# Two fused blocks on one core: rotary halves exchanged by DMA, q's root moved into the softmax's scale, low parts in four instructions

## What is computed

```python
def first_block(...):                 # 512 latent and 256 context tokens
    x, xc = rwkv7 layer               # scans in both directions, 16 heads of 64
    x = differential attention layer  # 8 heads, 2 x 64 wide, keys: 256 context + 512 latent
def second_block(...):                # two layers of hybrid_layer
    qa = rope(rms_norm_2(to_heads(a_q, 6), qk_g[0])) ...   # 6 window heads
    qb = rope(rms_norm_2(to_heads(b_q, 6), qk_g[2])) ...   # 6 dilated heads
    qm = rms_norm_2(to_heads(m_q, 4), qk_g[4])             # 4 memory heads, no rope, 256 keys
```

```python
def rope(x):                          # apply_axial_rope: the same in two groups of 2 x 16 channels
    x1, x2 = x[..., :half], x[..., half:]
    return concatenate([x1 * cos - x2 * sin, x2 * cos + x1 * sin])
```

## Time and profile before

| | |
|---|---|
| median of 3 runs | 2569.64 us (2568.6 to 2583.72) |
| profiled execution | 2575.68 us, span 2573.9 us |
| busy in the span | TensorE matmuls 2209.8, weight loads 1631.9, VectorE 1367.8, ScalarE 1156.6, GpSimd 679.5 us |
| mean granted TensorE clock | 0.936 of full |
| chain that ended last, by engine | PE 62%, DVE 15%, ACT 11%, issue 7%, POOL 3%, DMA 2% |
| a high part on ScalarE (line 238) | 128 times, mean 1052 ns |
| stages, about | `Mix` and `Scan` to 1200 us, `Mid` to 1344, `Diff` to 1775, first out-projection to 1857, pages to 2134, out-projection to 2230, pages to 2507, out-projection to 2573.9 |

### The profile page before, as it was taken

The page is one execution under the profiler, slowest core; times in us unless marked ns, Lnnn a source line. Parts: engine busy times, 40 slices in busy tenths (PEclk is TensorE's granted clock), DMA queues, the critical chain, the costliest instruction groups (busy, mean ns, idle before and its releaser), DMA issues.

```text
span 2573.9 us, 59035 instructions
## 1 busy us (share of the span) xinstructions
PE 2209.8 (86%) x25736; PEld 1631.9 (63%) x25736; DVE 1367.8 (53%) x2342; ACT 1156.6 (45%) x1933; POOL 679.5 (26%) x410
## 2 busy tenths in 40 slices
PE   8799999288888878876879999996899988899978
PEld 2587777167766767765667666654666665566656
DVE  1367878334444545454346566653456653466652
ACT  2466666233333334333244555453355553354552
POOL 0334453300011011013133222223433432433332
PEclk9899999599998999998889999997999998999998
DMA  7116362733332222214121111102111111111121
GB/s 269 64 50 184 117 184 84 209 113 106 84 95 79 59 75 57 61 38 159 58 87 60 34 42 40 50 25 83 59 65 50 58 58 66 66 58 58 50 66 66
DMA packets 148482, 211.32 MB, mean 82 GB/s; under 512 B 81921, under 2 KB 106753, under 8 KB 147457
## 3 DMA queue, kind: packets, MB, share of 16 engines
q1 hardware_dynamic: 137120, 164.28, 20.2%
q0 software_dynamic: 9952, 40.11, 5.1%
q10 hardware_dynamic: 1152, 3.15, 0.3%
HBM read 165.30 MB, written 42.21 MB: 81 GB/s over the span
## 4 chain that ended last, share of the span: by engine, by line
PE 62%; DVE 15%; ACT 11%; issue 7%; POOL 3%; DMA 2%; SPq 0%; ACTq 0%; DVEq 0%; POOLq 0%
PE ps L258 9%; PE ps L260 8%; PE ps L259 8%; PE ps L1332 3%; PE ps L538 3%; PE ps L1322 2%; PE ps L1347 2%; PE ps L2233 2%; PE ps L391 2%; PE ps L2729 2%; PE ps L2706 1%; DVE st L2292 1%; PE ps L311 1%; PE ps L1197 1%; DVE s L916 1%
## 5 line engine op out<-in xcount | busy, mean ns | idle before, releaser
L243 POOL TENSOR_TENSOR wbl<-wb,wbh 128x1024 fp32r<-128x1024 f32 x128 | 315.8, 2467 | 595.9 <-ACT wbh L238 591.1
L258 PE MATMUL ps<-hTh,wah 128*128 128x512 f32 (+1 forms) x512 | 181.0, 353 | 17.4 <-POOL wal L243 11.0
L258 PE MATMUL ps<-hT2h,wbh 128*128 128x512 f32 x416 | 181.5, 436 | 16.3 <-POOL wbl L243 8.9
L258 PE MATMUL ps<-hT1h,wbh 128*128 128x512 f32 (+1 forms) x432 | 176.5, 409 | 3.1 <-POOL hT1l L2372 3.1
L259 PE MATMUL ps<-hTl,wah 128*128 128x512 f32 (+1 forms) x512 | 175.1, 342 | 0.0
L260 PE MATMUL ps<-hTh,wal 128*128 128x512 f32 (+1 forms) x512 | 174.9, 342 | 0.0
L339 POOL TENSOR_TENSOR ro<-ro 128x256 f32<-128x256 f32 (+1 forms) x12 | 11.9, 993 | 582.9 <-DVE ro L323 582.9
L238 ACT ACTIVATE wbh<-wb 128x1024 fp32r<-128x1024 f32 x128 | 134.6, 1052 | 69.4 <-PE ps L1928 43.5
L260 PE MATMUL ps<-hT2h,wbl 128*128 128x512 f32 x416 | 164.2, 395 | 0.0
L259 PE MATMUL ps<-hT2l,wbh 128*128 128x512 f32 x416 | 163.8, 394 | 0.0
L243 POOL TENSOR_TENSOR wal<-wa,wah 128x1024 fp32r<-128x1024 f32 x34 | 102.1, 3004 | 219.7 <-ACT wah L238 219.7
(11 more groups left out here) (400 smaller groups left out, 5676.6 us busy)
## 6 DMA issues: line engine op xcount, KB each, us to landing
wb<-in_w_in SPq DMA_DIRECT2D x56, 512.0 KB, 3.4
s_str_dram<-s POOLq DMA_DIRECT2D x48, 576.0 KB, 8.7
wm<-in_ada SPq DMA_DIRECT2D x48, 512.0 KB, 4.6
bkv<-s_str_dram SPq DMA_DIRECT2D x96, 192.0 KB, 3.3
wa<-in_rw_in SPq DMA_DIRECT2D x34, 512.0 KB, 3.5
wb<-in_da_in SPq DMA_DIRECT2D x32, 512.0 KB, 3.4
ARI<-s_str_dram SPq DMA_DIRECT2D x96, 128.0 KB, 3.5
wb<-in_w_out SPq DMA_DIRECT2D x16, 512.0 KB, 3.4
```

The lines of the kernel that those rows point to most:

```text
L243: e.tensor_tensor(self.lo[:, n % 2], self.raw[:, n % 3], self.hi[:, n % 2].bitcast(F32), ALU.subtract).then_inc(self.K.s.w_lo, 1)
L258: e.matmul(z, wh[:, k, :], hi[:, k, a:b], start=k == 0, stop=False)
```

## The change

There are three parts.

1. **Exchange by DMA.** The 40 permutation products go. The channels of q and k are ordered on the host (`AXIAL`, applied to the weights and gains of `Diff`) so that partners are always 32 partitions apart, and the sign goes into the sine table. After the copy into `qb` or `kb`, SP issues four DMAs of 32 partitions each that write the partners into `tm`; VectorE multiplies `tm` by the sine in place. GpSimd's cosine product, which overwrites `qb` or `kb`, now waits for those DMAs. The issues stand in SP's stream after the loads of certain weight blocks.
2. **q's root in the softmax.** Except in dilated pairs, whose mask holds weights, q isn't multiplied by its root. The sums of squares are made with tokens on partitions: four matmuls, with `sq` as weights and two columns of `blk` (`K.halves`) moving, give a 128 x 8 tile. The root steps work on 8 columns (`rq`, `mq`) and the result is the scale of the exponential and of the negated maximum. The 1/8 goes into k's gain.
3. **Low parts in four.** Each low part of the 128 blocks of `W` is made by four GpSimd instructions of 128 x 256.

With two uses fewer a head has 11 bank uses and a rotary page 7. The diff, cut to its core:

```diff
+AXIAL = [32 * (p // 16 % 2) + 16 * (p // 32) + p % 16 for p in range(64)]
+        self.halves = self.con[:, CCOLS["blk"][0]:CCOLS["blk"][0] + 128:64]
 def split_lo(self, e, n):
-            e.tensor_tensor(self.lo[:, n % 2], self.raw[:, n % 3], self.hi[:, n % 2].bitcast(F32),
-                            ALU.subtract).then_inc(self.K.s.w_lo, 1)
+            w = 8 // self.pieces
+            for k in range(0, 8, w):
+                i = e.tensor_tensor(self.lo[:, n % 2, k:k + w, :], self.raw[:, n % 3, k:k + w, :],
+                                    self.hi[:, n % 2, k:k + w, :].bitcast(F32), ALU.subtract)
+            i.then_inc(self.K.s.w_lo, 1)
+def turn_halves(e, out, x, sem):
+    for a in range(0, 128, 32):
+        e.dma_start(out[a ^ 32:(a ^ 32) + 32, :], x[a:a + 32, :]).then_inc(sem, 16)
...
 # Diff
-            self.use += [E(1), E(2), M(0), E(3), N(1), E(4), M(1), M(2), E(5), N(2), E(6), t(1), t(2)]
+            self.use += [E(1), E(2), M(0), E(3), E(4), M(1), M(2), E(5), E(6), t(1), t(2)]
-        self.ra.pe(e, 3 * h, psum[:, self.take(e, i + 2), :], K.blk, self.sq[0][:, :])
+        bank = self.take(e, i + 2)
+        for qt in range(4):
+            m = e.matmul(psum[:, bank, 2 * qt:2 * qt + 2], self.sq[0][:, 128 * qt:128 * qt + 128], K.halves,
+                         start=True, stop=True)
+        m.then_inc(self.ra.ss, 1)
-        e.matmul(psum[:, self.take(e, i + 4), :], self.ac[:, 0:128], q[:, :], start=True,
-                 stop=True).then_inc(s.nr_rot, 1)
-        e.matmul(psum[:, self.take(e, i + 9), :], self.ac[:, 0:128], k[:, 256:768], start=True,
-                 stop=True).then_inc(s.nr_rot, 1)
+        if h >= 2:
+            e.wait_ge(s.sm_exp, 8 * (h - 1))
+        self.ra.act(e, 3 * h, psum[:, (i + 2) % 3, 0:8], self.rq[b][:, :], 1e-6, 64.0)
+    def sp_turn(self, e, h, z):
+        e.wait_ge(s.evac_a, self.ea0 + 6 * h + (3 if z else 1))
+        if h:
+            e.wait_ge(s.nr_sum, 2 * h + z - 1)
+        turn_halves(e, self.tm[z], self.kb[b][:, 256:768] if z else self.qb[b][:, :], self.exchanged(h, z)[0])
-            e.tensor_tensor(self.tm[z][:, :], psum[:, (i + use) % 3, :], sin, ALU.mult).then_inc(s.nr_sin, 1)
+            e.wait_ge(*self.exchanged(h, z))
+            e.tensor_tensor(self.tm[z][:, :], self.tm[z][:, :], sin, ALU.mult).then_inc(s.nr_sin, 1)
-        scaled(q, self.R[0], 0, 0)
 # GpSimd, before the cosine
-            e.wait_ge(s.nr_rot, 2 * h + z + 1)
+            e.wait_ge(*self.exchanged(h, z))
 # the softmax
-                             scale=0.125, bias=st[:, cc:cc + 1], accum_out=st[:, 2 + cc:3 + cc])
+                             scale=self.rq[b][:, 2 * qt + cc:2 * qt + cc + 1], bias=st[:, cc:cc + 1], accum_out=...)
-                e.tensor_scalar(st[:, cc:cc + 1], st[:, cc:cc + 1], -0.125, None, ALU.mult)
+                e.wait_ge(s.ra_r, self.ra.done(3 * h))
+                e.tensor_scalar(st[:, cc:cc + 1], st[:, cc:cc + 1], self.rq[b][:, 2 * qt + cc:2 * qt + cc + 1], -1.0,
+                                ALU.mult, ALU.mult)
 # SP, Diff
         for n in range(11, 43):
             self.W.load(e, n)
+            if 12 <= n < 42 and n % 4 < 2:
+                self.sp_turn(e, n // 4 - 3, n % 4)
...
 # Second: the same, with
-                self.use += [E(1), E(2), M(0), E(3), N(1), M(1), E(4), N(2), t]
+            self.use += [E(1), E(2), M(0), E(3), M(1), E(4), (s.tok_c, self.c0["tok_c"] + P + 1)]
+        if self.kind(P) == 1:
+            self.ra.pe(e, 2 * P, psum[:, bank, :], K.blk, self.sq[0][:, :])
+        else:
+            ...
+        for n in range(43, 128):
             self.W.load(e, n)
+            l, m = divmod(n - 52, 40)
+            if 0 <= m < 24 and m % 4 < 2:
+                self.sp_turn(e, 8 * l + m // 4, m % 4)
```

More of the change, by code:

```diff
@@ L2046, in pe_project @@
         for j, (a, c) in enumerate(((0, 4), (4, 6))):
-            bank = self.take(e, i + 11 + j)
+            bank = self.take(e, i + 9 + j)
             for z in range(a, c):
@@ L2531, in pe_project @@
         e.wait_ge(s.nr_sq, o["nr_sq"] + 2 * P + 1)
-        self.ra.pe(e, 2 * P, psum[:, self.take(e, i + 2), :], K.blk, self.sq[0][:, :])
+        bank = self.take(e, i + 2)
+        if self.kind(P) == 1:
+            self.ra.pe(e, 2 * P, psum[:, bank, :], K.blk, self.sq[0][:, :])
+        else:
+            for qt in range(4):
+                m = e.matmul(psum[:, bank, 2 * qt:2 * qt + 2], self.sq[0][:, 128 * qt:128 * qt + 128], K.halves,
+                             start=True, stop=True)
+            m.then_inc(self.ra.ss, 1)
         run(some(pk, 1))
@@ L2546, in pe_project @@
         run(pv)
[L2547 removed]
+        pg = self.pe_product(e, n + 3, self.hT, 512, i + 5)
         next(pg)
         yield
[L2550 to L2552 removed]
         e.wait_ge(s.evac_a, self.ea0 + 4 * P + 3)
[L2554 removed]
+        bank = self.take(e, i + 6)
         for z in range(w // 128):
@@ L2559, in pe_project, with roots @@
         yield
+    def roots(self, P):
+        if self.kind(P) == 1:
+            return self.sq[0][:, :], self.R[0][:, :], 512
+        return self.mq[:, :], self.rq[P % 2][:, :], 8
     def act_project(self, e, P):
@@ L2576, in square_evac @@
             e.activation(sq, m, ACT.Square).then_inc(s.nr_sq, 1)
-            e.activation(out, m, ACT.Copy, scale=K.Q("qkg", 6 * (P // 8) + 2 * self.kind(P) + z, 1)).then_inc(s.evac_a, 1)
+            g = 6 * (P // 8) + 2 * self.kind(P) + z
+            e.activation(out, m, ACT.Copy, scale=K.sm[:, 72 + g:73 + g] if z and self.kind(P) != 1 else
+                         K.Q("qkg", g, 1)).then_inc(s.evac_a, 1)
         if P % 8:
@@ L2626, in scaled @@
                 e.tensor_tensor(buf, buf, self.tm[z][:, :], ALU.add).then_inc(s.nr_sum, 1)
+            if z == 0 and self.kind(P) != 1:
+                return
+            if t:
                 e.wait_ge(s.nr_sum, o["nr_sum"] + v)
@@ L2642, in dve_project @@
         if t:
[L2643 removed]
+            turned(1)
         scaled(k[:, 0:w], 1)
```

214 lines of the change are left out of this document (111 added, 103 removed).

## The result

The changed kernel takes **2543.89 us** (median of 4 runs, 2541.42 to 2547.46) against 2570.49 for the kernel before (median of 4 runs): ratio 0.9886, 95% interval 0.987 to 0.9902. The forecast was 2510. The profiled execution took 2541.42 us with a span of 2539.6, which is 34.3 us less than the span of the profiled execution of before. Of these, 6.3 lie ahead of the read-out, in code that the change doesn't touch.

The account below looks back on a forecast made before the run. Heads and pages were taken as close to a matmul bound, with a few us of gaps each. Terms summed to -59.2 us, from 2575.68 to 2516.5 profiled, 2510 at the median; forecast range 2495 to 2528, wider range 2490 to 2544.

Parts of the forecast that it names:

- The rotary products: First attention and second block: 40 products of 0.86 us leave TensorE's own time, 34.4 us less.
- What replaces them: Four DMAs on SP's queue per exchange: 4.7 us against 9.4 us of cover at the tightest steady place, costed at nothing.
- rival 3: The exchange lands late: transfers follow each other, k lands 4.2 us beyond cover in 7 heads, 2539; chance 0.08.
- q's sums: In 8 heads and 10 pages one wide product becomes eight small records: 0.4 us more.
- q's root: Smaller root steps ahead of the row scaling: 8.8 us less in heads, 5.6 in window pages, 4.8 for pair 6.
- Low parts in four: Shorter holds of VectorE for pair 7, 5.7 us less with its root wait; six dearer blocks on the chain, 2.8 more.
- rival 4: Low parts become the bound as VectorE gets between the pieces, from 4.5 us a part upward: 2611; chance 0.06.
- Banks: The gate product takes another bank and no longer waits for the copy of v: 6.7 us less.
- Softmax with a scale in memory: Exponentials and negated maxima with a scale operand take 0.15 us longer for each exponential: 3.6 us more on the chain.
- (1): Only the work goes and the waits come back, as TensorE's turn also waits for a copy: 2540; chance 0.24.
- (2): More than the sum: an emptier VectorE also shortens copies and score waits, a further 15 to 20 us, 2492; chance 0.10.
- (5): q's root on PE's side stays where it is if small steps are fixed cost; no chance of its own.

Follow-up runs that it names:

- e4: The kernel before with only the low parts made in four operations: 2584.24 us against 2573.51, ratio 1.0043.
- e12: The changed kernel with q's root wide again in all heads and pages, exchange and low parts in four kept: 2569.09 us, ratio 0.9991.
- e6: The changed kernel with a useless product of the same length where q's rotary product stood in each head: 2543.78 us, heads 51.20.
- e7: The changed kernel with a useless product of the same length where k's rotary product stood in each head: 2551.03 us, heads 52.07.
- e2: The changed kernel with GpSimd's cosine product of q in heads 1 to 7 held until VectorE's second softmax difference: 2530.46 us, ratio 0.9842.
- e8: The changed kernel with the constant 0.125 as softmax scale, q's root computed but left out: 2537.56 us, ratio 0.9849, heads 50.47.
- e1: The changed kernel with each low part in one operation again: 2543.72 us, ratio 0.9884.
- e9: The changed kernel with GpSimd's cosine product of q and gate product held, and ScalarE's copy of turned probabilities moved forward: 2531.22 us, ratio 0.9842.

## Why the prediction was wrong, step by step

The sum was -59.2 us. The medians moved by 26.6, the profiled executions by 34.3. From first to last it is 26.4, so some 33 are missing. The table gives them in three groups. Rotary products and banks were to bring 41.1 and bring 17.8 (e4 to e12). Low parts in four, with their gain for pair 7, were to be even and cost 11.0 (before to e4). q's root with the softmax was to bring 18.4 and brings 19.6 (e12 to the changed kernel). By parts, in the order of the prediction:

**The rotary products** (-34.4 forecast). This is the step that failed: "They stand inside the product stream and wait for nothing, so what they take is TensorE's own time." For the pages that the table lists it holds: 1.7 us less in each page of a rotary pair (e4 to e12), the 2 x 0.86 of the earlier trace rows. For the heads it doesn't. A product that waits for nothing may still stand between two instructions whose distance others set. q's did (e6), and removing it opened a wait of 1.38 us where there had been one of 0.3. k's gave its 0.82 (e7).

**What replaces them** (nothing forecast). The transfer costs nothing in the steady heads and pages: 2.0 to 2.4 us from issue to landing in the median, below my lower end of 3.4, and four overlap; rival 3 falls. The trace's groups of DMA issues:

```profile
tmc<-qc SPq DMA_DIRECT2D x48, 64.0 KB, 2.4
...
tma<-kb SPq DMA_DIRECT2D x32, 64.0 KB, 2.0
```

That is close to the fixed 2 us which the Trainium skill, page "SBUF — State Buffer", section "The DMA setup-cost knee (why "@ 1 MiB" ≠ asymptote)", gives for small transfers, paid once, not four times. But I asked only whether it lands too late. It lands early, and so GpSimd's cosine product no longer waits the 5.4 us for TensorE and runs onto VectorE's row scaling: 0.90 us a head (e2). With q's product giving nothing and k's giving 0.8, that leaves the heads where they were: 7 x 1.9 = 13 us of the forecast are missing here. VectorE does wait for an exchange at three places that are not steady: 4.6 us in head 0, behind the two tables, and 2.7 in all in the first pages of the two layers. No run shows what these cost.

**q's sums** (+0.4) were right in size: eight records take 0.80 us in the chain of waits, 0.10 each, nearer to the turn's 0.11 than to the 0.14 of the modulation. A timeline row of a head:

```profile
1530.18 0.95 PE L2030 MATMUL ps<-con,sqa 128*128 128x2 f32 x8
```

**q's root** (-8.8, -5.6, -4.8, and 2.8 of the -5.7 for pair 7) came out near for heads and windows. From e12 to the changed kernel a head loses 1.20 us (forecast 1.25) and the page of pair 2 loses 1.31 (1.4). Pair 6 loses 0.6 and 2.4 (2.4 each): in the first layer the lower clock comes late and the low part is waited for for 3.4 us, in the second for 1.6. Pair 7 loses 1.9 and 1.5. These differences hold the dearer exponentials too, and so the agreement in the heads is partly luck. Between e12 and e8, which both have the constant scale, the root alone brings 1.98 us a head, 1.5 for pair 2 and 25.9 from first to last, against the 22.0 of the four terms. Two terms were too small, and they nearly cancel. Together with the exponentials the part brings 19.6 us from first to last, most of the result.

**Low parts in four** (the other 2.9 of the -5.7, and +2.8). The gain is there where I put it, but smaller (0.5 to 0.9 us for each pair 7 in e4). The price is mis-sized: "six stand on the chain". In e4 it is 0.4 us in each head, 0.45 in each page and 4.6 in the stretches outside of both, 11 us in all after the gain. Against rival 4 I had held that low parts "have several us to spare in a page"; the trace had 0.05. In the changed kernel they pay for themselves in the pages through the shorter hold on VectorE, and the whole is as with whole low parts (e1).

**Banks** (-6.7). The wait for the copy of v went as forecast, 0.5 us a page, and brought next to nothing. In window and dilated pages a second low part now ends last before that product, and TensorE waits 0.45 us for it. The text said "a later bank that is late instead"; it was the weights.

**Softmax with a scale in memory** (+3.6). The exponential grew by 0.09 us (902 to 992 ns) and VectorE's small step by 0.06 (154 to 214), as costed. They count more than twice as much in a head as I let them, 0.77 us in place of 0.3, and 6.3 us from first to last in place of 3.6 (e8).

The rivals: (1) gave 2540 and is nearest to what came, with its mechanism for the heads, the turn that waits for a copy behind the softmax. Its other half, that small roots bring nothing, is wrong, and its sum keeps the whole 34.4 for the rotary products, so its number is near by luck. (2), (3), (5) didn't occur. (4) has the right place and a smaller price: a low part takes 2.8 us undisturbed, 3.07 in the mean, and up to 4.56 where VectorE gets between the operations; three of 128 pass the 4.5 from which it was to decide. Of the marks named, heads over 50.5 us had been set as the sign of a wrong prediction, and they came in at 51.25.

What stays open: why the lower clock falls early in some pages of pair 6 and late in others, with the same instructions; and what head 0's late exchange costs.

## What to carry to other kernels

Work taken from the bounding engine is worth its time only where that engine's neighbours on the path are its own: measure the distance between the two waits around it, or put an idle instruction of the same length there. When a step is freed from a wait, look where it will run now and beside what, above all between VectorE and GpSimd; a wait that puts it back costs one line. And a dependency without a row in the table of waits can have no slack at all: compare the end of the producer with the start of the consumer before making the producer 0.4 us longer.

## What the runs showed of the hardware

VectorE instructions with operands in SBUF were stretched by a GpSimd instruction beside them, from 1.02 to 1.93 us and from 0.62 to 1.27, and GpSimd's too, from 1.29 to 1.62. The stretch vanished where the two were put one behind the other (e2, e9). Cutting one GpSimd instruction of 2.42 us into two makes 2.64 (2 x 1.32 in the mean), into four 3.20 (4 x 0.80). The operations overlap a little: from the first start to the last end four take 3.07 in the mean, 2.8 when VectorE is quiet and up to 4.56 when it isn't. An exchange of partition halves inside SBUF, four DMAs of 64 KB, is issued in 2.4 to 3.3 us on SP and lands 2.0 to 2.4 us (medians) after each issue. In the page of pair 6, 3.4 us at TensorE's lower clock cost up to 2 us more behind a wait than ahead of it.
